# A copy from one DRAM tensor to another, moved behind 64 gathers on the same queue

## Time and profile before

| what | value |
|---|---|
| median of three runs | 2248.11 us (2240.42 to 2248.68) |
| the profiled execution, its own time | 2249.93 us |
| its span, first to last instruction | 2248.3 us |
| PE busy over the span | 96% |
| first stage | to about 216.5 us |
| mean granted TensorE clock | 0.982 |

### The profile page before, as it was taken

The page is one execution under the profiler, slowest core; times in us unless marked ns, Lnnn a source line. Parts: engine busy times, 40 slices in busy tenths (PEclk is TensorE's granted clock), DMA queues, the critical chain, the costliest instruction groups (busy, mean ns, idle before and its releaser), DMA issues. The chain is left out here.

```text
span 2248.3 us, 32767 instructions
## 1 busy us (share of the span) xinstructions
PE 2155.8 (96%) x12394; PEld 1592.3 (71%) x12394; DVE 1023.5 (46%) x1933; ACT 573.8 (26%) x1252; POOL 1110.1 (49%) x1063
## 2 busy tenths in 40 slices
PE   9898899999999999989999999999999999999997
PEld 6676555466777777767777667676767777777776
DVE  5342677336341233057788655555541254213412
ACT  2102577502000000025556343434410100000011
POOL 3212456256664357275577452525345476535652
PEclk9999799999999999999999999999999999999998
DMA  9826000832221221151222424333222122112211
GB/s 331 233 75 199 1 1 1 306 115 73 75 75 75 76 82 69 75 184 57 61 85 81 110 57 135 94 98 95 95 92 100 75 74 76 75 75 75 75 76 42
DMA packets 125911, 216.45 MB, mean 96 GB/s; under 512 B 73602, under 2 KB 96002, under 8 KB 109762
## 3 DMA queue, kind: packets, MB, share of 16 engines
q1 hardware_dynamic: 119234, 197.13, 26.4%
q0 software_dynamic: 3088, 14.03, 1.8%
q10 hardware_dynamic: 3440, 3.25, 0.4%
HBM read 185.08 MB, written 37.55 MB: 99 GB/s over the span
## 5 line engine op out<-in xcount | busy, mean ns | idle before, releaser
L2014 PE MATMUL ps<-xn,ring 128*128 128x288 f32 x768 | 198.9, 407 | 5.4 <-DVE xn L2117 3.2
L2014 PE MATMUL ps<-hid,ring 128*128 128x288 f32 x768 | 192.8, 406 | 0.0
L2014 PEld LDWEIGHTS ps<-xn,ring 128*128 128x128 f32 x768 | 145.3, 190 | 48.3 <-DVE xn L2117 5.9
L2014 PEld LDWEIGHTS ps<-hid,ring 128*128 128x128 f32 x768 | 145.6, 190 | 40.6 <-ACT p L2051 0.7
L2097 POOL TENSOR_TENSOR prod<-prod,rstd 128x1152 f32<-128x1152 f32 x32 | 83.9, 2623 | 179.5 <-DVE prod L2181 163.2
L2051 ACT ACTIVATE p<-ps 128x288 f32<-128x288 f32 x48 | 19.8, 412 | 597.3 <-PE ps L2014 597.3
L3740 PE MATMUL ps<-xn,ring 128*128 128x288 f32 x512 | 147.2, 422 | 4.1 <-PE ps L3848 2.0
L1122 POOL TENSOR_SCALAR ring<-ring,fac 128x128 f32<-128x128 f32 (+2 forms) x96 | 92.4, 978 | 86.1 <-DVE fac L1551 86.1
L2014 PE MATMUL ps<-x_sum,wsum 128*128 128x288 f32 x512 | 130.6, 407 | 3.4 <-DVE x_sum L2121 1.9
L2071 POOL TENSOR_TENSOR wsum<-ring 128x512 f32<-128x512 f32 x64 | 81.9, 1280 | 99.0 <-DMA ring<-in_w_mlp 91.2
L2014 PE MATMUL ps<-hid_sum,wsum 128*128 128x288 f32 x512 | 128.4, 407 | 0.2
(11 more groups left out here) (602 smaller groups left out, 4594.3 us busy)
## 6 DMA issues: line engine op xcount, KB each, us to landing
ring<-in_w_mlp SPq DMA_DIRECT2D x64, 1024.0 KB, 4.8
ring<-in_w_gdn_in SPq DMA_DIRECT2D x16, 1024.0 KB, 4.8
ring<-in_w_nsa_in SPq DMA_DIRECT2D x9, 1024.0 KB, 18.7
ring<-in_w_gdn_z SPq DMA_DIRECT2D x8, 1024.0 KB, 4.9
x<-in_seq_state SPq DMA_DIRECT2D x4, 2048.0 KB
out_seq_state<-x SPq DMA_DIRECT2D x4, 2048.0 KB, 6.8
ring<-in_w_gdn_out SPq DMA_DIRECT2D x8, 1024.0 KB, 4.9
out_win_old<-in_win_rows POOLq DMA_DIRECT2D x1, 8064.0 KB, 46.0
```

Source lines behind the costliest of these rows:

```text
L2014: mm = nc.tensor.matmul(S.ps[:, base + BANK[p], 0:HT], stationary(p, blk.units[pair // 4], pair % 4), moving(blk.kind, p, pair), start=pai ...
```

## The change

The copy is issued by the same engine on the same queue, but behind the 64 gathers of kinds 0 and 1, and behind two waits for their landings. All else stays, including the gathers of kinds 2 and 3 that come after it on POOL and SP's wait at L605.

```diff
         def _(pool):
             setup_gpsimd(pool, S, setup, sq)
             pool.wait_ge(first_mm, 1)
-            pool.dma_start(S.out["win_old"], S.dram["win_rows"][:, TD:, :]).then_inc(copied, 16)
             pool.wait_ge(S.pages_in, 16)
             for u in range(2):
                 if u == 1:
...
                         pool.dma_start(pages(u)[:, bass.ds(n * NPG + j, 1)],
                                        S.dram["cache_cmp"][u, bass.ds(page, 1)].rearrange("a p t -> p a t")
                                        ).then_inc(early[u], 16)
+            for u in range(2):
+                pool.wait_ge(early[u], 16 * NPG * NSEQ)
+            pool.dma_start(S.out["win_old"], S.dram["win_rows"][:, TD:, :]).then_inc(copied, 16)
             pool.wait_ge(d.product, 7 * (NB - 1))
             late_pages(pool, 2, (1,), early_rows[1])
             pool.wait_ge(product, 2)
```

## The result

| | kernel before | changed kernel |
|---|---|---|
| median | 2247.53 us (2240.42 to 2250.08, 6 runs) | 2256.87 us (2254.06 to 2259.74, 6 runs) |
| ratio to the kernel before | | 1.0049, 95% interval [1.0037, 1.0061] |
| profiled execution, own time | 2249.93 us | 2257.1 us |
| its span | 2248.3 us | 2255.5 us |
| mean granted TensorE clock | 0.982 | 0.982 |

The change makes the kernel slower by about 11 us by the ratio (8.3 to 13.7 us by its interval) and by 7.2 us between the two profiled executions; the two medians lie 9.3 us apart. The forecast was 2253.5 us, 5.4 us slower.

The account below looks back on a forecast made before the run. PE bounds the kernel, with a 9.57 us stall at unit 4 blamed on the copy. Removing it gains 9.6 us, SP's held gathers lose 15.0, so 2248.1 + 5.4 = 2253.5 us, range 2238 to 2263 (8 in 10).

Parts of the forecast that it names:

- What bounds the kernel: First stage: the early copy delays unit 4's weights on PE; 9.57 us lost, 6.46 of it waiting, some 3.0 slower products.
- Rival 3: Unit 4's stall stays, caused by bias tables and saved x; the late copy costs 15 us: 2263 us, chance 0.06.
- Eight engines, 2.4 us a packet, one packet of each queue in turn: Copy on the DMA engines: 8 of 16 busy, 2.42 us per 64.5 KB packet, other queues' small packets each waiting one out.
- When the copy is issued: POOL, after the gathers of kinds 0 and 1: last gather at 129, added waits end at about 131.7.
- The excess of 16 us in the page-number reads: POOL's first 15 gathers of kind 1: slow page-number reads during bias-table stores, assumed to stay in the changed kernel.
- When it lands: Copy's end: 38.7 us at least, 43 taken, so landed at 174.7, bounds 153 to 179.
- Which issues it holds: Kind 2's gathers: SP's L399 held until the copy lands and backlog clears; SP free at 180, kind 3 at 203.1.
- 3 us of backlog and 2.3 us for L398 and L399: SP after the copy's landing: allowance for queue backlog and these two issues before SP is free at 180.
- PE does nothing between, the slow clock is the same: PE before kind 3: idle through the lateness; 3 us of slower clock in that group both before and after.
- Rival 2: ACT's page issues held, only 8 of 16 accepted; activation at 188, +13 us, about 2262 us; chance 0.17.
- Rival 1: Copy lands by 159.7, all of it hidden, the 9.57 us gain stays: 2238.5 us, chance 0.28.
- The sum: Whole kernel: 9.6 us gained at the front, 15.0 lost late, +5.4 us on median 2248.1: 2253.5 us.

Follow-up runs that it names:

- 16-engine version: Changed kernel with the late copy cut into 16 pieces per sequence, pieces as slowest dimension, same bytes: 2239.84 us, ratio 0.9971.
- the kernel that did issue its last gather at 114: Changed kernel with the Toeplitz bias table cut to one of 16 heads, in its four stores (L381) and its read (L398): 2234.65 us, ratio 0.9955.
- the kernel with the small read: Changed kernel with L398 reading one of 16 heads of the Toeplitz bias table, stores and copy unchanged: 2246.88 us, ratio 1.0006.

## Why the prediction was right, and where it was off

- **What bounds the kernel: right.** The stall at unit 4 was the copy's: with it gone, there is no wait, and the gain is 9.57 us by the timeline (9.63 by the kernel with no copy). Unit 5 starts at 81.07 and kind 2's gathers at 150.4, where 81.8 and 151.0 were named. Rival 3 is refuted.
- **Eight engines, 2.4 us a packet, one packet of each queue in turn: right as far as the runs show.** The share of 51.3% on a quiet stretch and the 16-engine version show the first two. The third is not shown engine by engine; the 13 and 14 small packets in 4 us are what it expects. The rule of the Trainium skill in "DMA: Bandwidth & Descriptors", section on why a DMA increments its semaphore by 16, agrees with the 16-piece version too: with 16 pieces outermost all 16 engines are busy.
- **When the copy is issued: right, within 1.1 us** (132.8 for 131.7). The excess of 16 us in the page-number reads stayed (130.04 against 114.27 without the stores), and for the cause named. In the kernel before the reads were slow in kind 1, since the stores were held back there; now they are slow in kind 0.
- **When it lands: right** (175.9 for 174.7; 1.1 of the 1.2 us come from the issue). The lower bound of 153 was 114 and 38.7 us of packets, without the 2.7 us from the last gather to the copy's issue; the kernel that did issue its last gather at 114 landed its copy at 162.9.
- **Which issues it holds: right for SP, incomplete for ACT.** SP is free at 182.75 where 180.0 was predicted: 1.2 us come from the landing, and 1.55 us from the term "3 us of backlog and 2.3 us for L398 and L399", which measured 6.85 us. This is the mis-sized term. From there to kind 3 it was 23.8 us for 23.4. The prediction also lost 0.3 us in adding up: 180.0 + 23.4 is 203.4, not 203.1. Kind 3 starts at 206.54, and the late loss is 17.8 us for 15.0.
- **PE does nothing between, the slow clock is the same: half right.** Kind 3's group took 10.16 us for 10.88 before, but kind 2's took 2.7 us more, at a granted clock that averages 0.73 from 180.7 us on. That costs nothing here, since kind 3's data came 6 us after it.
- **Rival 2 was half true.** ACT stood, as the rival said: its tenth page's issue was held (the rival took 8 as accepted), and its first activation began at 180.4, not at 188. The hold ended at about 162.0 + 10.4 = 172.4, 3.5 us ahead of the landing, and only six issues at 1.24 us followed, where the rival had eight behind the landing. In the kernel with the small read ACT alone still costs 8.3 of the 17.8 us. The forecast's own mechanism, SP's hold, delays the attention stage by 9.5 us beyond that and sets the time.
- **Rival 1 fell by its condition.** It needed a landing by 159.7. The experiments put that bound at about 158, and every kernel that met it, by an earlier issue or half the bytes, came out at 2237 to 2238 us, where 2238.5 had been worked out. The fit of the Trainium skill for a POOL-issued DMA ("DMA: Bandwidth & Descriptors", section on the anatomy of one DMA) gave this copy an estimate of 21 us; eight engines took 43.1 us and sixteen 27.2, so no run here reaches it.
- **The sum: the way and the mechanism were right, the size too small.** The prediction's +5.4 us stands against +7.2 us between the profiled spans (8.2 us at the start of the attention stage), against +9.3 us between the medians and against +11.0 us, 8.3 to 13.7, by the ratio. The terms above account for 2.8 us of the difference. For most of the rest there is a reason that the numbers suggest and no run tests: the profiled execution of the kernel before is 2.4 us above its median, that of the changed kernel 0.2 us above its own, and the prediction took a difference of timelines for a difference of medians, which holds to a few us only. That 2253.5 us came within 3.4 us of the measured median, with the change itself 5.6 us too small by the ratio, is in part luck: the median of three runs to which it was added, 2248.1, lies above the mean of the six, 2246.0.

## What to carry to other kernels

A big DRAM-to-DRAM copy occupies as many engines as its slowest dimension gives it, each in long packets, and whatever else stands on those engines gets on by about one small packet for each long one: count when it lands, and put that beside the next moment at which another queue must be drained, because a blocked issue stops all that stands behind it on SP and ACT. Moving such a copy can just move the collision; here two edits removed it, 16 outermost pieces in the old place (ratio 0.9946, interval [0.9933, 0.996]) and the unchanged copy in an empty stretch (0.9951, [0.9937, 0.9965]), which these runs can't tell apart. And before moving work behind a loop of small issues, check what sets that loop's pace: 16 us of it were reads slowed by another engine's stores.

## What the runs showed of the hardware that was not expected

- A register read of a page number takes 0.29 us by its median and about 2 us behind a store of the bias tables. Over 64 gathers that moved the last one from 114.27 to 130.04, and putting the data into partition 64 made no difference.
- Two copies of the same shape issued 0.7 us apart ran side by side, at 72 packets in 14 us against 48, and a quarter more bytes cost 3.1 us. One copy kept 8.2 engines busy, by its shape, but the next on the same queue went on idle ones.
- A packet of 64.5 KB took 2.4 us with eight engines at work and 3.1 us with sixteen, so the copy went 1.6 times as fast, not twice.
- Beside the copy ACT's queue took nine pages of 64 KB before an issue was held, and SP's took eight pages and a part of what follows. The first of these pages had landed by then (4.3 us after its issue), so this is not the number that a queue holds at once.
- With eight of the engines under the copy, an issue of ACT was held for 10.43 us and one of SP for 16.42 us, where they take 0.35 us and 1.83 us without it.
